# Expert matrices in 16 KB runs and 2 MB loads, with no wait between loads, in a hybrid encoder layer with a mixture of experts

## The reference

```python
mod = (silu(c) @ w_ada + b_ada)          # shift, scale, gate for both halves
h = rmsnorm(x, ln1_g) * (1 + scale1) + shift1
x = x + gate1 * token_mixer(h, w_in, w_out, ...)    # conv, Fourier, spatial gating
h = rmsnorm(x, ln2_g) * (1 + scale2) + shift2
probs = softmax(h @ router_w); sel = probs + router_b
# one of 8 groups for each token, then the top two experts e in it, weights gw
y = sum over the two: gw * ((silu(h @ w1[e]) * (h @ w3[e])) @ w2[e])
x = x + gate2 * y;  out = rmsnorm(x, final_g)
```

## Time and profile before

| | |
|---|---|
| time, median of 3 runs | 1831.21 us (1820.58 to 1837.73) |
| span of the profiled execution | 1837.1 us (the nearest of the runs' times: 1837.73) |
| busy share PE, DVE, ACT, POOL | 66%, 25%, 12%, 10% |
| mean granted clock of TensorE | 0.819 of full speed |
| mixing and routing | 0 to about 510 us |
| expert stage | about 510 to 1790 us |
| tail | to the end, about 47 us |
| bytes moved | 517.73 MB, mean 282 GB/s |

### The profile page before, as it was taken

How to read it: one execution, slowest core, us unless ns; L and a number is a source line. 1 busy time by engine, 2 the same in 40 slices (tenths; PEclk the granted TensorE clock), 3 DMA queues, 4 the chain that set the end, 5 groups by cost and what they waited for, 6 DMA issues and landing times.

```text
span 1837.1 us, 31943 instructions
## 1 busy us (share of the span) xinstructions
PE 1213.9 (66%) x12648; PEld 643.2 (35%) x12649; DVE 456.3 (25%) x880; ACT 215.1 (12%) x537; POOL 186.7 (10%) x322
## 2 busy tenths in 40 slices
PE   4999999999377457765545786465645368544860
PEld 3544546455234224332223443232323134222430
DVE  1399762235511001110000111010001011100116
ACT  1300132112010001010000110000000001000104
POOL 3011200000011001010000111010001001100113
PEclk7999999999688779787777898787768679766885
DMA  9454704531988999898899899998989999999967
GB/s 338 155 206 138 278 0 161 181 102 61 385 313 305 336 339 325 314 316 313 329 318 336 311 325 313 328 336 301 341 302 337 331 331 322 342 351 324 327 225 277
DMA packets 156232, 517.73 MB, mean 282 GB/s; under 512 B 11865, under 2 KB 28777, under 8 KB 156072
## 3 DMA queue, kind: packets, MB, share of 16 engines
q1 hardware_dynamic: 130176, 471.05, 71.3%
q0 software_dynamic: 12032, 32.33, 5.2%
q10 hardware_dynamic: 13992, 13.90, 2.2%
HBM read 482.22 MB, written 35.01 MB: 282 GB/s over the span
## 4 chain that ended last, share of the span: by engine, by line
DMA 69%; PE 25%; DVE 3%; issue 1%; ACT 1%; SPq 0%; POOL 0%; POOLq 0%; ACTq 0%; DVEq 0%
DMA arena<-in_exp_w 65%; PE banks L547 8%; PE banks L625 6%; PE banks L575 2%; PE banks L593 2%; DMA arena<-xh_dram,where 1%; PE banks L681 1%; PE banks L495 1%; DMA arena<-in_w_ada 1%; DMA ys_dram<-arena 1%; DMA arena<-in_x 1%; PE banks L641 1%; PE banks L692 1%; DVE arena L1249 0%; DVE arena L1244 0%
## 5 line engine op out<-in xcount | busy, mean ns | idle before, releaser
L681 PE MATMUL banks<-arena 128*32 128x256 f32 x6784 | 484.8, 448 | 462.3 <-DMA arena<-in_exp_w 430.1
L681 PEld LDWEIGHTS banks<-arena 128*32 128x32 f32 x6784 | 242.9, 128 | 671.8 <-issue 574.6
L692 PE MATMUL banks<-arena 128*32 128x256 f32 x3392 | 220.4, 403 | 37.2 <-DVE arena L1219 37.0
L1213 DVE TENSOR_TENSOR arena<-arena,banks 128x128 f32<-128x128 f32 x106 | 30.8, 290 | 760.3 <-ACT arena L842 758.8
L547 PE MATMUL banks<-arena 128*128 128x512 f32 x352 | 155.6, 600 | 4.0 <-ACT arena L782 4.0
L692 PEld LDWEIGHTS banks<-arena 128*32 128x32 f32 x3392 | 108.9, 114 | 108.4 <-issue 50.2
L444 POOL COPY where<-quarters 128x1 int32 (+1 forms) x108 | 19.9, 184 | 1234.6 <-ACT arena L856 1070.0
L1219 DVE TENSOR_TENSOR arena<-banks,arena 128x256 f32<-128x256 f32 x106 | 45.1, 426 | 360.0 <-DMA ys_dram<-arena 310.9
L842 ACT ACTIVATE arena<-banks 128x128 f32<-128x128 f32 x106 | 29.6, 279 | 872.5 <-PE banks L681 749.3
L969 DVE SCALAR_TENSOR_TENSOR arena<-arena 128x1024 f32<-128x1024 f32 x90 | 115.6, 1285 | 3.2
L447 POOL DMA_INDIRECT arena<-xh_dram,where x108 | 104.8, 970 | 87.7 <-POOL where L444 81.7
(11 more groups left out here) (201 smaller groups left out, 661.0 us busy)
## 6 DMA issues: line engine op xcount, KB each, us to landing
arena<-in_exp_w SPq DMA_DIRECT2D x384, 1024.0 KB, 7.1
arena<-in_w_ada SPq DMA_DIRECT2D x12, 2048.0 KB, 11.2
ys_dram<-arena ACTq DMA_DIRECT2D x106, 128.0 KB
ys_dram<-arena POOLq DMA_DIRECT2D x16, 512.0 KB, 10.2
arena<-in_x SPq DMA_DIRECT2D x2, 2048.0 KB, 20.8
arena<-in_dft SPq DMA_DIRECT2D x1, 4096.0 KB, 12.4
arena<-in_w_out SPq DMA_DIRECT2D x1, 4096.0 KB, 14.0
arena<-in_x SPq DMA_DIRECT2D x8, 512.0 KB, 4.2
```

Of the source, the lines that this page charges most:

```text
L681: last = pe.matmul(h_p[32 * q:32 * q + 32, 0:2 * P].rearrange("p (a b) -> p a b", a=2), xt_s[:, k % 2, k // 2, :], w13[:, :, k, q * P:(q + ...
L692: last = pe.matmul(y_p[32 * q:32 * q + 32, 0:QUART], ff_t[:, k * BLK:(k + 1) * BLK], w2[:, k, q * QUART:(q + 1) * QUART], start=(k == 0), ...
```

## The change

1. `AHEAD` and its waits are gone. In the loop, SP issues one load for each matrix (`matrix`): w1 and w3 after `s_h13`, w2 after `s_yp`.
2. A load's run is now 16 KB a partition. Partition p holds rows 8p to 8p + 7 of w1 and w3 and rows 4p to 4p + 3 of w2. The first four experts are loaded by `piece` in halves of 8 KB runs.
3. As w2's rows now lie 4p + k, the up products read w1 and w3 with a column step of four, so that hidden value 4m + q stands in column m of group q.
4. The feature order of h follows (chunk k holds features 8p + k): `w_in`, `router_w` and the column vectors are loaded in one transfer each for four, the first four modulation products read with a step of four, and the x transposes with a step of eight. The scaled rows for `xh_dram` are written in the old quarter order by an instruction that reads x2 in pairs (line 1142).

```diff
         def d_cols(vector):
-            return vector.rearrange("(q p j) -> p q j", q=4, j=2)
+            return vector.rearrange("(p k) -> p k", k=CH)
...
         def chunk(view, k):
+            return view[:, k:D:CH]
+
+        def quarter_chunk(view, k):
             first = QUART * (k // 2) + k % 2
             return view[:, first:first - k % 2 + QUART:2]
...
-                for q in range(4):
-                    sp.dma_start(w_in_s[:, 2 * q:2 * q + 2, f0:f1],
-                                 w_in[q * QUART:(q + 1) * QUART, f0:f1].rearrange("(p j) f -> p j f", j=2)
-                                 ).then_inc(s_win[part], 16)
+                sp.dma_start(w_in_s[:, :, f0:f1], w_in.rearrange("(p k) f -> p k f", k=CH)[:, :, f0:f1]).then_inc(s_win[part], 16)
...
             def piece(e, slot, k):
                 u, h = k // 2, k % 2
                 if u < 2:
-                    src = (exp_w1, exp_w3)[u][bass.ds(e, 1), h * 512:(h + 1) * 512, :].rearrange("e (q p j) f -> (e p) q (j f)", q=2, j=2)
+                    src = (exp_w1, exp_w3)[u][bass.ds(e, 1), :, :].rearrange("e (p h c) f -> (e p) h (c f)", p=P, h=2)[:, h, :]
...
+            def matrix(e, slot, u):
+                if u < 2:
+                    src = (exp_w1, exp_w3)[u][bass.ds(e, 1), :, :].rearrange("e (p c) f -> (e p) (c f)", p=P)
+                else:
+                    src = exp_w2[bass.ds(e, 1), :, :].rearrange("e (p k) d -> (e p) (k d)", p=P)
+                sp.dma_start(at(slot * EXPERT_FLOATS + u * 4096, 4096), src).then_inc(s_w[slot][u], 16)
...
-                    for k in range(6):
-                        if k == 0:
-                            sp.wait_ge(s_h13, end)
-                        if k == 4:
-                            sp.wait_ge(s_yp, end)
-
-                        before, rounds = (slot, r + 2) if k >= AHEAD else ((slot - 1) % SLOTS, r + (2 if slot else 1))
-                        sp.wait_ge(s_w[before][(k - AHEAD) % 6], rounds * 16)
-                        piece(r * SLOTS + (SLOTS + slot), slot, k)
+                    sp.wait_ge(s_h13, end)
+                    for u in range(2):
+                        matrix(r * SLOTS + (SLOTS + slot), slot, u)
+                    sp.wait_ge(s_yp, end)
+                    matrix(r * SLOTS + (SLOTS + slot), slot, 2)
...
+                        columns = ada_s[:, n % 2, k, q:HALF:4] if n < 4 else ada_s[:, n % 2, k, q * P:(q + 1) * P]
...
-                                         w13[:, :, k, q * P:(q + 1) * P], start=(k == 0), stop=(k == CH - 1), tile_position=(0, 32 * q))
+                                         w13[:, :, k, q:FF:4], start=(k == 0), stop=(k == CH - 1), tile_position=(0, 32 * q))
...
-                    for k in range(4):
-                        pe.wait_ge(s_w[slot][k], (r + 1) * 16)
+                    for u in range(2):
+                        pe.wait_ge(s_w[slot][u], (r + 2) * 16)
...
-                    v.tensor_scalar(xr[:, i % 4, :], x2[:, i % 4, :], rstd[:, 1, i:i + 1], None, ALU.mult).then_inc(s_xhat, 1)
+                    v.tensor_scalar(xr[:, i % 4, :].rearrange("t (q p j) -> t q p j", q=4, j=2),
+                                    x2[:, i % 4, :].rearrange("t (p q j) -> t q p j", q=4, j=2),
+                                    rstd[:, 1, i:i + 1], None, ALU.mult).then_inc(s_xhat, 1)
```

More of the change, by code:

```diff
@@ L42 @@
 EARLY = 4
-AHEAD = 2
 NEG = -3.0e38
@@ L181, in d_cols @@
         def d_cols(vector):
-            return vector.rearrange("(q p j) -> p q j", q=4, j=2)
-        def d_tile(view):
-            return view.rearrange("p (q j) -> p q j", q=4)
+            return vector.rearrange("(p k) -> p k", k=CH)
         def chunk(view, k):
+            return view[:, k:D:CH]
+        def quarter_chunk(view, k):
             first = QUART * (k // 2) + k % 2
@@ L213, in build @@
         s_zeros, s_yzero = sem("zeros_ready"), sem("result_rows_zeroed")
-        s_w = [[sem(f"slot{i}_{what}_in") for what in ("w1a", "w1b", "w3a", "w3b", "w2a", "w2b")] for i in range(SLOTS)]
+        s_w = [[sem(f"slot{i}_{what}_in") for what in ("w1", "w3", "w2")] for i in range(SLOTS)]
         s_xrow, s_xcopy = sem("block_rows_in"), sem("block_rows_moved")
@@ L317, in piece @@
                 if u < 2:
-                    src = (exp_w1, exp_w3)[u][bass.ds(e, 1), h * 512:(h + 1) * 512, :].rearrange("e (q p j) f -> (e p) q (j f)", q=2, j=2)
+                    src = (exp_w1, exp_w3)[u][bass.ds(e, 1), :, :].rearrange("e (p h c) f -> (e p) h (c f)", p=P, h=2)[:, h, :]
                 else:
-                    src = exp_w2[bass.ds(e, 1), h * 256:(h + 1) * 256, :].rearrange("e (k p) d -> (e p) k d", k=2)
-                sp.dma_start(at(slot * EXPERT_FLOATS + k * 2048, 2, D), src).then_inc(s_w[slot][k], 16)
+                    src = exp_w2[bass.ds(e, 1), :, :].rearrange("e (p h k) d -> (e p) h (k d)", p=P, h=2)[:, h, :]
+                sp.dma_start(at(slot * EXPERT_FLOATS + k * 2048, 2048), src).then_inc(s_w[slot][u], 16)
+            def matrix(e, slot, u):
[4 more added lines that the diff above has]
+                sp.dma_start(at(slot * EXPERT_FLOATS + u * 4096, 4096), src).then_inc(s_w[slot][u], 16)
             for k in range(2):
@@ L405, in _ @@
             for n, vec in ((LN1, ln1_g), (LN2, ln2_g)):
-                pool.dma_start(d_tile(col[:, n, :]), d_cols(vec)).then_inc(s_cols, 16)
+                pool.dma_start(col[:, n, :], d_cols(vec)).then_inc(s_cols, 16)
             for n, m in ((BSH1, 0), (BSC1, 1), (BSH2, 3), (BSC2, 4)):
-                pool.dma_start(d_tile(col[:, n, :]), d_cols(b_ada[m * D:(m + 1) * D])).then_inc(s_cols, 16)
+                pool.dma_start(col[:, n, :], d_cols(b_ada[m * D:(m + 1) * D])).then_inc(s_cols, 16)
             for h in range(6):
                 pool.dma_start(bs_b[64 * (h % 2):64 * (h % 2) + 64, h // 2, :], sgu_b[h, :].partition_broadcast(64)).then_inc(s_small, 16)
-            for q in range(4):
-                pool.dma_start(router_s[:, 2 * q:2 * q + 2, :], router_w[q * QUART:(q + 1) * QUART, :].rearrange("(p j) e -> p j e", j=2)
-                               ).then_inc(s_rb, 16)
+            pool.dma_start(router_s, router_w.rearrange("(p k) e -> p k e", k=CH)).then_inc(s_rb, 16)
             pool.dma_start(router_bb, router_b.partition_broadcast(P)).then_inc(s_rb, 16)
@@ L425, in _ @@
             for k, m in ((SH2, 3), (SC2, 4)):
-                pool.dma_start(d_tile(col[:, k, :]), d_cols(mod_dram.ap()[m * D:(m + 1) * D])).then_inc(s_modcols, 16)
+                pool.dma_start(col[:, k, :], d_cols(mod_dram.ap()[m * D:(m + 1) * D])).then_inc(s_modcols, 16)
             pool.wait_ge(s_ss, TILES)
@@ L478, in ada_columns @@
                 pe.wait_ge(freed_d, freed_at[index[("ada", n)]][1])
-                for q in range(2):
+                half = 64 * (n % 2)
+                for lane in range(4):
                     for j in range(2):
[L481 to L484, removed]
+                        k = 4 * j + lane
+                        last = pe.matmul(ps[half:half + 64, k:k + 1], head_rows[:, n, j:P:2], ident[:, 32 * lane:32 * lane + 1],
+                                         start=True, stop=True, skip_group_check=True)
                 last.then_inc(filled, 1)
@@ L494, in ada @@
                     for q in range(4):
-                        last = pe.matmul(ps[32 * q:32 * q + 32, 0:P], c_wide[:, k, :], ada_s[:, n % 2, k, q * P:(q + 1) * P],
+                        columns = ada_s[:, n % 2, k, q:HALF:4] if n < 4 else ada_s[:, n % 2, k, q * P:(q + 1) * P]
+                        last = pe.matmul(ps[32 * q:32 * q + 32, 0:P], c_wide[:, k, :], columns,
                                          start=(k == 0), stop=(k == CH - 1), tile_position=(0, 32 * q))
@@ L561, in _ @@
                     if g == index[("g", 0, 0)]:
-                        pe.wait_ge(s_win[0], 64)
+                        pe.wait_ge(s_win[0], 16)
                     if key[1] == 0:
@@ L568, in _ @@
                 elif kind == "b":
-                    pe.wait_ge(s_win[1], 64)
+                    pe.wait_ge(s_win[1], 16)
                     z_cols(ps, 2 * CONV + key[1] * P, key[2])
                 elif kind == "v":
-                    pe.wait_ge(s_win[2], 64)
+                    pe.wait_ge(s_win[2], 16)
                     i = key[1]
@@ L577, in _ @@
                 elif kind == "u":
-                    pe.wait_ge(s_win[3], 64)
+                    pe.wait_ge(s_win[3], 16)
                     z_cols(ps, 1024 + key[1] * P, key[2])
@@ L630, in _ @@
                     for j in range(4):
-                        last = pe.transpose(ps[:, j * P:(j + 1) * P], chunk(xr[:, i % 4, :], 4 * h + j), ident)
+                        last = pe.transpose(ps[:, j * P:(j + 1) * P], quarter_chunk(xr[:, i % 4, :], 4 * h + j), ident)
                     last.then_inc(filled, 1)
@@ L635, in _ @@
                     if i == 0:
-                        pe.wait_ge(s_rb, 80)
+                        pe.wait_ge(s_rb, 32)
```

(8 more changed lines are left out.)

## The result

The changed kernel takes 1,949.1 us (median of 4 runs, 1,939.1 to 1,955.1), the kernel before 1,834.5 in the same job. The ratio is 1.062, 95% interval 1.057 to 1.068: 115 us slower, where the forecast was 50 us. The profiled execution's span is 1,947.1 us, at a mean granted clock of 0.897 (before: 0.819).

The account below looks back on a forecast made before the run. The prediction took the throttled queue of expert loads as the bound, with the block's store taking over. 1,837 + 50 (store) + 1 (mixing) = 1,888, or 1,882 us against the median; range 1,750 to 1,995, the forecast's own 1,838 to 1,925 (chance 0.52).

Parts of the forecast that it names:

- Part 3: Up products reading w1 and w3 with a step of four: cost taken as nothing, bounds nothing or a doubling of 3.66 us a block.
- Rival (a): Step-of-four read halves the up products' rate: 7.3 us each, 30 blocks pay in full, +110, 1,992 us; chance 0.24.
- Part 2: Block's store behind 16 KB load packets takes 23 to 25.6 us; 38 blocks held, expert stage 1,330 us, 50 more.
- Part 1: Expert loads with longer runs and no throttle: 14.8 us an expert against 20.8, alone a gain of over 300 us.
- Part 4: Mixing stages, with fewer loads, stepped modulation and transpose reads and x-hat read in pairs: taken as +1 us.
- (b): Stores mostly fall outside loads, or 16 KB packets let others between; DMA engines bound the stage: 1,659 us, chance 0.13.
- (c): The queue cuts the runs into 4 KB pieces again, so only the throttle is gone: 1,688 us, chance 0.06.
- the list of what would show it: Signs: 16 KB packets, stores near 25 us, L1219 idle many times 311 us, little L681 idle, DMA gaps, up product 3.66 us.

Follow-up runs that it names:

- Run 11: The kernel before with w1 and w3 read with a column step of two: 1,833.4 us in one execution, beside 1,838.7 for the kernel before.
- run 2: The kernel before with only the up products' read of w1 and w3 changed to a step of four: 1,871.3 us, ratio 1.025.
- run 1: The changed kernel with the up products reading 128 neighbouring columns again in place of the step of four: 1,887.1 us, ratio 1.032.
- run 6: The changed kernel with contiguous up reads and its loop loads issued as 1 MB halves with 8 KB runs: 1,786.3 us, ratio 0.972.
- run 4: The kernel before without each load's wait for the load before the last, runs still 4 KB: 1,708.0 us, ratio 0.935.
- run 7: The changed kernel with contiguous up reads and each 2 MB load waiting for the load two before it: 1,869.9 us, ratio 1.016.
- run 3: The changed kernel with the block's store written partitions outermost, on 16 DMA engines in place of four: 1,658.0 us, ratio 0.907.
- run 10: The changed kernel with only the block's store split into four stores of 32 partitions, result kept: 1,715.0 us, ratio 0.938.
- Run 5: The changed kernel with contiguous up reads and the block's store on 16 DMA engines: 1,570.6 us, ratio 0.854.
- run 8: The kernel before without the wait between loads, and with four stores of 32 partitions a block: 1,589.2 us, ratio 0.864.
- run 9: The changed kernel with w2 in 4 KB runs, contiguous up reads and four stores of 32 partitions a block: 1,584.8 us, ratio 0.867.

## Why the prediction was right and wrong

**The step that failed is Part 3: "I take nothing" for the step of four.** The term was set at 0, at one end of its own bounds; measured, an up matmul goes from 379 to 632 ns and the 64 of a block from 3.66 to about 7.5 us, close to the other end, and the time by some 60 us. The argument was that a step of two costs a tenth at most, taken from the stationary loads of the earlier trace rows. Run 11 shows that this was true (3%), and run 2 that it said nothing of a step of four: the cost isn't in proportion to the step but sets in somewhere above two (a step of three wasn't run). The second argument, that an fp32 matmul takes its columns slowly enough for any read, was wrong as well. The Trainium skill ("SBUF — State Buffer", Door 1) asks for at least two hits on each line of 16 bytes; the runs agree: two fp32 of a line at a step of two are nearly free, one at a step of four is not. The same passage gives 4 fp32 as how far one can stride for free; taken as a step of four, the 632 ns contradict it, and the measurement decides. Rival (a), the first of the three (Part 3 calls it the second), was that case, and it was priced at +110 from 30 blocks that pay in full. 7.3 us an up product was near, but 60 us are the worth of 16 blocks (at 3.8): by the account of run 1 the rest is covered by waits for the store, more of it than was allowed for.

**Part 2 held, in mechanism and size.** The store beside 16 KB packets was forecast at 23 to 25.6 us and took 24.4; with 8 KB packets (run 6) some 15.2. Runs 4 and 7 remove the rival that depth counts, runs 3 and 10 show that 32 packets on each of four engines are the reason. Its sum is near what run 1 measures: +64 us over its job's kernel before (58 by the ratio) for +51 forecast; that the times, 1,887 and 1,882, are closer still is in part luck, as the kernel before was 8 us lower in that job. The sum counted 38 held blocks; in run 1's chain 33 stores took 22.8 to 24.9 us. Run 1's stage went from 511.9 to 1,838.1 (last store issued), 1,326 us, for the 1,330 taken as the middle of 1,287 and 1,373.

**Part 1's gain is real and was not to be had in this kernel.** Run 5 moves 415 GB/s and takes 1,571 us. The gain comes from the wait that is dropped (run 4: 4 KB packets, -116 us) and from the store mended behind it (run 8, ratio 0.864 for 0.935); the longer runs add 1% at most (runs 5, 8 and 9). What the mended store is worth with the wait kept was not tried.

**Part 4**, +1: the first up product starts at 512.3 us for 510.3. Run 2, whose mixing stages are those of before, has it at 513.2, so these 2 us show no cost. The first four modulation products, which read with a step of four too, pay the same kind of price: a matmul of 128 columns takes 410 ns at the median and 272 in the later products, whose columns are contiguous. These products take 3.8 to 3.9 us each where they took 3.3 to 3.6, with nothing of it to be seen in the start of the stage. The gather of a block's rows lands after 6.9 us for 6.2, a little less than the 0.9 to 1.4 more that Part 2 gave, and under the store. Of SP's issues in the loop one in two goes (360 become 180), not "2 issues of 3"; nothing hung on that.

**Rivals (b) and (c)** fell by the packets: 16 KB ones, and the engine lets only one of them ahead of each small packet. (What (c) calls "the same DMA page" of the Trainium skill is "DMA: Bandwidth & Descriptors"; its preference for packets of at most 4096 B cut no run here.) (b)'s point of decision, a block's cycle of 10.7 us beside loads, was right to name: in run 3 it is 9.9 to 10.3, and the kernel is faster. Of the list of what would show it, three came true: the packets (27,310 on SP's queue from 510 to 1900, for 99,343 from 510 to 1790), no wait of L681 for `in_exp_w`, and gaps in the strip. Two came true in part: 22 stores of the changed kernel's chain took 23.7 to 24.7 us and most others 11 to 20, and L1221's wait for the store is twice 311 us (2.6 times in run 1), not many times. The up product's 3.66 us did not.

## What to carry to other kernels

Before loads are made longer or let run free, look for the small transfer that something waits for, and multiply the packets that it has on its busiest engine by the time of one large packet; if its pattern begins with a short dimension, reorder or split it first. A moving fp32 operand read with a step of two cost next to nothing here, with a step of four a block's up products took twice the time: where a layout asks for a step of four, keep the old layout. What a dearer instruction costs is read from the idle time of its own engine, which covered five sixths of it here; it costs more once the wait that covered it is mended.

## What the runs showed of the hardware

With the step of four, TensorE's clock made no difference to the up matmul. Ahead of the changed kernel's first up product PE stood idle for 9.3 and, after two transposes, for 1.6 us; in that product the granted clock goes from the lower level (0.50, 1.2 GHz) to full (2.4 GHz). Two windows of it, and the up matmuls to 515.0 and from 515.9 on:

```profile
512.20:514.00 1.80, 1.74 (x16) 0.74 (x20) 0.00 (x0) 0.00 (x0) 0.00 (x0) 0.50 0.79 330
...
516.00:518.00 2.00, 2.00 (x24) 0.67 (x20) 0.00 (x0) 0.83 (x1) 0.96 (x1) 0.99 0.05 10
```

```profile
L681 PE MATMUL banks<-arena x27: 630/632/640, 512.3 to 515.0; 128*32 128x256 f32 x27
...
L681 PE MATMUL banks<-arena x32: 630/633/662, 515.9 to 519.1; 128*32 128x256 f32 x32
```

The contiguous one of the kernel before takes 379 ns at full clock; its first ones, at a granted clock of 0.50, took:

```profile
L681 PE MATMUL banks<-arena x16: 628/634/635, 510.3 to 511.6; 128*32 128x256 f32 x16
```

At the lower level the step of four is free, at full clock it takes all that the clock would give. So the higher mean clock of the changed kernel (0.897 for 0.819), which came with a PE busy for 80% of the span, gave its up products nothing.

A store with `q` outermost takes ACT 554 ns to issue, the same bytes with 128 rows outermost 343 ns. The store on four engines took 3.3 us alone, 11.0 beside 4 KB packets, some 15.2 beside 8 KB and 24.4 beside 16 KB.
